# Seven-product down projection: order of low parts, buffers of the third pair, order of the final rows

## The reference

```
h = rms_norm(x, g_pre_ffn)
f = (silu(h @ w_gate) * (h @ w_up)) @ w_down      # 1024 -> 2816 -> 1024
x = x + rms_norm(f, g_post_ffn)
```

## Time and profile before

| | |
|---|---|
| median of 3 runs | 1016.67 us (1016.48 to 1016.77) |
| the profiled execution | 1015.4 us |
| its span, first to last instruction | 1013.2 us |
| mean granted TensorE clock | 0.997 |
| busy: TensorE / VectorE / GpSimd / ScalarE | 988.4 / 671.8 / 472.5 / 401.5 us |

### The profile page before, as it was taken

One profiled execution on the slowest core, in us unless ns is written; L12 is line 12 of the kernel. 1 busy time (PEld: TensorE's weight loads), 2 busy tenths in 40 slices (PEclk: granted clock), 3 DMA queues, 4 the chain that ended last, 5 costly groups with the idle time before them and its releaser, 6 DMA issues.

```text
span 1013.2 us, 19111 instructions
## 1 busy us (share of the span) xinstructions
PE 988.4 (98%) x7694; PEld 793.9 (78%) x7694; DVE 671.8 (66%) x1046; ACT 401.5 (40%) x760; POOL 472.5 (47%) x495
## 2 busy tenths in 40 slices
PE   6998999999999999999999999999999999989997
PEld 5786777777777777777778888888888888878885
DVE  4799796566466955556548881366655566689897
ACT  4134432321323335445555444443223223254563
POOL 3376457244335766656774447534444444400000
PEclk9999999999999999999999999999999999999999
DMA  9344533122224554213024648243333333245452
GB/s 261 87 135 138 121 87 71 24 65 63 66 64 115 161 143 125 64 32 85 23 65 129 188 135 255 60 146 104 92 94 103 96 91 103 82 138 172 138 178 92
DMA packets 149446, 111.31 MB, mean 110 GB/s; under 512 B 21189, under 2 KB 132047, under 8 KB 149368
## 3 DMA queue, kind: packets, MB, share of 16 engines
q1 hardware_dynamic: 145644, 104.16, 35.4%
q10 hardware_dynamic: 3692, 6.07, 2.2%
q0 software_dynamic: 32, 0.00, 0.0%
HBM read 99.70 MB, written 10.52 MB: 109 GB/s over the span
## 4 chain that ended last, share of the span: by engine, by line
PE 90%; DVE 5%; DMA 2%; issue 1%; POOL 1%; ACT 1%; SPq 0%; DVEq 0%; ACTq 0%
PE ps L2027 36%; PE ps L1977 7%; PE ps L1976 7%; PE ps L1975 7%; PE ps L2041 4%; PE ps L2145 3%; PE ps L2508 3%; PE ps L2510 3%; PE ps L2509 3%; PE ps L2390 3%; PE ps L2332 2%; PE ps L2416 1%; PE ps L2414 1%; PE ps L2415 1%; DMA XTOK<-in_x 1%
## 5 line engine op out<-in xcount | busy, mean ns | idle before, releaser
L703 POOL TENSOR_TENSOR WLO<-WRAW,WHI 128x1024 fp32r<-128x1024 f32 (+1 forms) x92 | 205.5, 2235 | 223.3 <-ACT WHI L817 223.2
L2027 PE MATMUL ps<-HLO,WHI 128*128 128x512 f32 x440 | 178.4, 405 | 0.0
L2027 PE MATMUL ps<-HHI,WHI 128*128 128x512 f32 x440 | 175.6, 399 | 1.0 <-DVE HLO L1316 0.7
L817 ACT ACTIVATE WHI<-WRAW 128x1024 fp32r<-128x1024 f32 (+1 forms) x91 | 85.9, 945 | 193.4 <-PE ps L1977 121.4
L1975 PE MATMUL ps<-HHI,WHI 128*128 128x512 f32 x336 | 131.1, 390 | 0.0
L1977 PE MATMUL ps<-HHI,WLO 128*128 128x512 f32 x336 | 130.7, 389 | 0.0
L1976 PE MATMUL ps<-HLO,WHI 128*128 128x512 f32 x336 | 130.7, 389 | 0.0
L2027 PE MATMUL ps<-HHI,WLO 128*128 128x512 f32 x440 | 118.1, 397 | 0.7 <-issue 0.7
L707 POOL CAST WHI<-WRAW 128x256 fp32r<-128x256 f32 (+1 forms) x133 | 62.9, 473 | 106.7 <-PE ps L2027 106.7
L738 POOL TENSOR_TENSOR WLO<-WRAW,WHI 128x256 fp32r<-128x256 f32 x132 | 105.8, 801 | 10.7
L2027 PEld LDWEIGHTS ps<-HHI,WHI 128*128 128x128 f32 x440 | 82.6, 188 | 23.0 <-issue 4.4
(11 more groups left out here) (451 smaller groups left out, 2006.5 us busy)
## 6 DMA issues: line engine op xcount, KB each, us to landing
WRAW<-in_w_in SPq DMA_DIRECT2D x47, 512.0 KB, 4.1
WRAW<-in_w_gate SPq DMA_DIRECT2D x22, 512.0 KB, 3.8
WRAW<-in_w_up SPq DMA_DIRECT2D x22, 512.0 KB, 3.9
WRAW<-in_w_down SPq DMA_DIRECT2D x19, 512.0 KB, 3.5
spilled<-SQ SPq DMA_DIRECT2D x24, 256.0 KB, 2.4
GATES<-spilled SPq DMA_DIRECT2D x6, 768.0 KB, 4.8
WRAW<-in_w_in SPq DMA_DIRECT2D x16, 256.0 KB, 3.7
WRAW<-in_w_branch SPq DMA_DIRECT2D x32, 128.0 KB, 2.9
```

The lines of the kernel that those rows point to most:

```text
L703: return pool.tensor_tensor(lo[:, 0:chunks, :], WRAW[:, n % NRAW, 0:chunks, :], hi[:, 0:chunks, :].bitcast(F32), ALU.subtract)
L817: act.activation(split_of(n)[0][:, 0:width_of(n), :], WRAW[:, n % NRAW, 0:width_of(n), :], ACT.Copy).then_inc(w_hi, 1)
L2027: last = pe.matmul(DB[g % 2][:, :], (wlo if which == "low" else whi)[:, c, :], lo if which == "x_low" else hi, start=a == 0, stop=a == 3 * ...
```

## The change

Five edits:

- The tile SQ moves behind SSUM in memory. The first buffer of RAWX (r = 4, 10, 16) then lies over RINV and SSUM, the second (r = 5, 11, 17) over SQ. Load r = 4 waits for `ff_gate` 22 (the last use of RINV) and r = 5 for `ff_hid` 21, in place of `ff_hid` 22 for both.
- GPF is loaded behind r = 12, not r = 6.
- VectorE makes the low parts of pair i ahead of `weight_sums(i + 1)`; `hidden_low(10)` goes behind the low parts of pair 2.
- ScalarE does a small Sqrt into two unused columns in round i = 4 of the second pass.
- The final rows: VectorE makes one row's gain product just ahead of that row's end, and takes the bias of t = 0 and 1 from the first square; ScalarE squares P1 before UC for t = 0, and UC before P1 for t = 1.

```diff
--- before.py
+++ after.py
@@ -290,9 +290,9 @@
     MISC = per.take("MISC", [P, 96])
     RINV_AT = per.at
     RINV = per.take("RINV", [P, T])
-    SQ = per.take("SQ", [P, 2, T])
     SSUM_AT = per.at
     SSUM = per.take("SSUM", [P, T])
+    SQ = per.take("SQ", [P, 2, T])
     WRAW = per.take("WRAW", [P, NRAW, 8, P])
     WHI = per.take("WHI", [P, NSPL, 8, P], F32R)
     WLO = per.take("WLO", [P, NSPL, 8, P], F32R)
@@ -656,7 +656,7 @@
                 if r < NRAW:
                     sp.wait_ge(w_lo, DN0 - NRAW + r + 1)
                 elif r < RAW1:
-                    sp.wait_ge(ff_hid, NF)
+                    sp.wait_ge(*((ff_hid, NF - 1) if r % 2 else (ff_gate, NF)))
                 else:
                     sp.wait_ge(x_lo, r - RAW1 + 1)
                     if r % 2:
@@ -666,7 +666,7 @@
                         .then_inc(raw_sem(r), 16)
                 else:
                     sp.dma_start(down_raw(r)[:, 0, :], w_down[(f + 1) * P:(f + 2) * P, T:D]).then_inc(raw_sem(r), 16)
-                if r == RAW1:
+                if r == 2 * RAW1:
                     sp.dma_start(GPF[:, :], bass.AP(par1.tensor, par1.offset + P * PAR["g_post_ffn"], [[0, P], [1, D]]))\
                         .then_inc(gpm_in, 16)
             for i in range(NPAIR):
@@ -1206,6 +1206,7 @@
                         act.wait_ge(uc_ok, 5 + a)
                         act.wait_ge(o_sq, 8 + a)
                         square(UC[:, 2 + a, :], 2 + a)
+                    act.activation(MISC[:, 70:72], EPSC, ACT.Sqrt)
 
             def row_std(t, bias, count):
 
@@ -1219,14 +1220,20 @@
                 act.wait_ge(o_sq, 8 + 2 + a)
                 square(OTOK[:, 2 + a, T:D], 6 + a)
                 row_std(2 + a, 2, 3 + a)
-            for a in range(2):
-                act.wait_ge(uc_ok, 8 + a + 1)
-                act.wait_ge(o_sq, 8 + 4 + 2 * a)
-                square(UC[:, a, :], a)
-                act.wait_ge(p_full, 6 + 2 * a)
-                act.wait_ge(o_sq, 8 + 5 + 2 * a)
-                square(P1[a][:, :], 4 + a)
-                row_std(a, 3 + a, 6 + 2 * a)
+            act.wait_ge(p_full, 6)
+            act.wait_ge(o_sq, 8 + 4)
+            square(P1[0][:, :], 0)
+            act.wait_ge(uc_ok, 8 + 1)
+            act.wait_ge(o_sq, 8 + 5)
+            square(UC[:, 0, :], 4)
+            row_std(0, 3, 6)
+            act.wait_ge(uc_ok, 8 + 2)
+            act.wait_ge(o_sq, 8 + 6)
+            square(UC[:, 1, :], 1)
+            act.wait_ge(p_full, 8)
+            act.wait_ge(o_sq, 8 + 7)
+            square(P1[1][:, :], 5)
+            row_std(1, 4, 8)
 
 
         @block.vector
@@ -1862,12 +1869,13 @@
                     pair_low(3)
                 hidden_sums(i)
             weight_sums(2)
-            hidden_low(NPAIR - 1)
             for i in range(2, NPAIR):
+                pair_low(2 * i)
+                pair_low(2 * i + 1)
+                if i == 2:
+                    hidden_low(NPAIR - 1)
                 if i + 1 < NPAIR:
                     weight_sums(i + 1)
-                pair_low(2 * i)
-                pair_low(2 * i + 1)
                 if i % 2 and i >= 3:
                     second_low((i - 3) // 2)
 
@@ -1937,22 +1945,41 @@
             dve.wait_ge(p_full, 3 + 1)
             for a in range(2):
                 dve.tensor_tensor(OTOK[:, 2 + a, T:D], P7[a][:, :], UC[:, a, :], ALU.add).then_inc(uc_ok, 1)
-            for a in range(2):
+            def scaled_c21(a):
+
                 dve.wait_ge(uc_ok, 6 + a + 1)
                 dve.tensor_tensor(OTOK[:, 2 + a, 0:T], OTOK[:, 2 + a, T:D], GPF[:, 0:T], ALU.mult).then_inc(ox_ok, 1)
-            final_row(0, 2)
-            final_row(1, 3)
-            for a in range(2):
+
+            def c12(a):
+
                 dve.wait_ge(p_full, 5 + 2 * a)
                 dve.tensor_tensor(UC[:, a, :], P5[a][:, :], UC[:, a, :], ALU.add).then_inc(uc_ok, 1)
                 dve.wait_ge(uc_ok, 8 + a + 1)
                 dve.tensor_tensor(OTOK[:, a, T:D], UC[:, a, :], GPF[:, T:D], ALU.mult).then_inc(ox_ok, 1)
-                dve.wait_ge(o_sq, 8 + 5 + 2 * a)
+
+            def scaled_c11(a, squares):
+
+                dve.wait_ge(o_sq, 8 + squares)
+                dve.tensor_tensor(OTOK[:, a, 0:T], P1[a][:, :], GPF[:, 0:T], ALU.mult).then_inc(ox_ok, 1)
+
+            def bias_of_row(a, squares):
+
+                dve.wait_ge(o_sq, 8 + squares)
                 dve.scalar_tensor_tensor(out=FBIAS[:, a:a + 1], in0=FSS[:, a:a + 1], scalar=1.0 / D, in1=FEPS[:, a:a + 1],
                                          op0=ALU.mult, op1=ALU.add).then_inc(o_bias, 1)
-                dve.wait_ge(o_sq, 8 + 6 + 2 * a)
-                dve.tensor_tensor(OTOK[:, a, 0:T], P1[a][:, :], GPF[:, 0:T], ALU.mult).then_inc(ox_ok, 1)
-                final_row(2 + a, a)
+
+            scaled_c21(0)
+            final_row(0, 2)
+            scaled_c21(1)
+            final_row(1, 3)
+            c12(0)
+            bias_of_row(0, 5)
+            scaled_c11(0, 5)
+            final_row(2, 0)
+            c12(1)
+            bias_of_row(1, 7)
+            scaled_c11(1, 8)
+            final_row(3, 1)
 
 
         @block.tensor
```

## The result

Five runs of the changed kernel gave a median of 1011.54 us (1009.20 to 1012.33), five of the kernel before 1016.48 us (1015.79 to 1016.77): a ratio of 0.9946, 95% interval 0.9934 to 0.9958. The kernel is 4.9 us faster; 5.2 was forecast, 1011.5 as the time.

The account below looks back on a forecast made before the run. TensorE, busy 988.4 of 1013.2 us, was taken as the bound. The terms -5.0 (stop and slow clock), +1.0 (new stop) and -1.2 (tail) sum to -5.2 us, so the median becomes 1011.5 us, range 1010.0 to 1013.2.

Parts of the forecast that it names:

- The stop at pair 2: First pass of the down projection: TensorE stands 3.26 us, then slow matmuls cost 1.74; 5.0 us in all, to be removed.
- Order and loads: First pass: VectorE's new order with earlier loads lets TensorE start pair 2 on time, giving the whole 5.0 us.
- The margin at pair 3: First pass: TensorE could start pair 3 at 912.23 and wants to at 912.97, so 0.74 us to spare.
- The early Sqrt: Second pass: its table load makes VectorE 1.56 us late, and TensorE stops 1.0 us before the last P7 product.
- The drain: ScalarE's table switch: the skill page's drain, up to 1380 ns, would make the stop 2.4 us and the sum -3.8.
- Rival B: Second pass: the early table switch costs double, TensorE's stop is 2.3 us, the time 1012.8 us; chance 0.12.
- The final rows: Tail after TensorE's last product: last output at 1010.56 instead of 1010.78, 0.2 us won; 1.2 without the added TensorE stop.
- the new stop: Second pass: TensorE waits 1.0 us before the last P7 product because of the early table load.
- The clock after a stop of 1.0: Second pass: nothing added for the clock, as an earlier 2.07 us gap left it at 1.00; a fall would give 1013.1.
- A side reading: In working out the loads, the prediction said GpSimd has no work after 888.
- The time: Whole kernel: the median of 1016.67 us becomes 1011.5, the old profiled execution lying 1.27 below that median.

## Why the prediction was right

- **The stop at pair 2 costs 5.0, standing and slow clock.** Right: order and loads together take 5.00 off the stage.
- **Order and loads.** The prediction worked out the order with the early loads in place and gave the whole 5.0 to it, without saying what either would give alone. The experiments divide it: the order does nearly all, the loads fill in the last 0.37. They are what keeps pair 3 from being 0.26 late. The margin at pair 3 (0.74 forecast) was 0.73: its first low part ended at 913.46, with the hand-over 913.59, and TensorE was due there at 914.32.
- **The early Sqrt costs TensorE 1.0.** Right in place, cause and size (0.97; a slower restart, which the sum left out, adds 0.08). That it costs as much as it saves stood in the sum only as 1.0 against 1.2; without it the stage is the same to 0.1 us.
- **The drain.** The Trainium skill ("ScalarE: Activation LUTs", What ACT_TABLE_LOAD costs) has 1283 ns for a load, which the traces show, and a drain of 1380 ns with it, which they don't: 0.03 us before the load, 0.01 behind it, and the stage grew by 1.49 us for a whole further load with its activation. Rival B falls with this.
- **The final rows win 1.2, or 0.2 with the new stop.** Right: 2.97 us from TensorE's end to the last output (3.03 forecast). The prediction didn't say how much of the 1.2 is the load and how much the new order, and no run settles it.
- **The clock after a stop of 1.0.** It stayed up, as forecast; the reason given (one gap of 2.07 with no fall) was weaker than I took it for. The first line of the earlier trace rows couldn't show it: the changed kernel also has 1.00 from 89 to 92 us, and the clock fell right behind, as the last section shows.
- **A side reading was off.** GpSimd's last instruction in the kernel before begins at 887.16 and takes 2.41 us, so its work ends near 889.6 and not by 888. No term of the sum uses it.
- **The time.** 1011.5 against 1011.54 is nearer than the method deserves, and partly luck. The runs spread over 3 us, the 1.27 us by which the old profile lay below its median was added whole, and the gain over the runs timed beside it was 4.9 and not 5.2. What the steps can vouch for is the stage, 5.2 forecast and 5.20 measured.

## What to carry to other kernels

An engine that feeds the bound engine should make what is wanted next before what is wanted later, even where all of it has to be made: here the order of four instructions on VectorE was worth 4.6 us, and earlier loads 0.4 on top. Taking a fixed cost out of the tail only pays if its new place is idle and nothing without slack hangs on it; the same table load gave nothing in round 4 and 1.0 us behind the loop, some 19 us later in the stage. To price such a move, follow the delayed engine to the next wait of the bound engine and look for idle time on the way: where there is none, the whole delay arrives, less what the bound engine itself had to spare (here 1.5 us of delay, 0.56 spare, a stop of 0.97).

## What the runs showed of the hardware

The same instructions ahead of the down projection took 896.3 to 899.0 us in these ten traces. Part of the spread is TensorE's clock. Every execution has a gap of 2.07 to 2.08 us around 90 us; in three of the ten the clock fell to half for 3.4 us behind it, in seven it did not. Here it did, in the changed kernel's first profile:

```profile
89.00:92.00 3.00, 0.92 (x8) 0.83 (x8) 2.76 (x4) 0.63 (x1) 3.00 (x2) 1.00 0.00 0
92.00:96.00 4.00, 4.00 (x15) 3.35 (x14) 4.00 (x2) 2.00 (x2) 3.61 (x2) 0.57 0.65 178
```

In the kernel before it did not (its stretch from 89 to 92 is in the earlier trace rows):

```profile
92.00:96.00 4.00, 4.00 (x23) 3.41 (x21) 4.00 (x2) 2.01 (x2) 3.89 (x2) 1.00 0.58 174
```

Little of that fall reached the stage. The slow matmuls put TensorE back by 1.5 to 1.6 us, but near 99 us the seven others stand still for 0.93 to 0.98 us and these three do not, and by 102 us 0.3 us is left of it. More came from the start of one trace, that with two early loads: its matmuls came at half the pace, 0.427 us apart, until 18.5 us, and it was 1.8 us behind the others from there on. What makes up the rest, in steps of about 0.3 us between 180 and 300 us, was not looked for and stays open.

The stops of 3.26 and 3.45 us in the stage brought the clock down both times, those of 0.26 to 1.46 in none of five traces. The Trainium skill ("TensorE: Matmul & The Clock Gate", What's actually happening) has idleness bring the clock down; the traces agree in so far as all five falls ahead of TensorE's end came behind a gap or stop of 2.07 us or more. They don't show why the same gap was followed by one in three executions and by none in seven. A single profile therefore can't say whether a gap of 2 us is followed by slow matmuls.
